# Routed experts: turns of 128 and of 64 slots one by one, two to a loop body

## The chip, the cores and the metric

The kernel runs on one core of a Trainium2 chip. Its engines are TensorE (PE; PEld are its weight loads), VectorE (DVE), ScalarE (ACT), GpSimd (POOL) and SyncE (SP), each with a queue of its own that it works through in order; sixteen DMA engines move data for all of them. The metric is the device time of one execution in microseconds (us).

## What is computed

Two blocks in fp32 on 256 tokens of width 1024. The part at hand is the expert layer of the first block: each token goes to its two best experts of eight, with a gate, an up and a down matrix of 1024 x 3584, 1024 x 3584 and 3584 x 1024 each.

```python
def swiglu(x, w_gate, w_up, w_down):
    return (jax.nn.silu(x @ w_gate) * (x @ w_up)) @ w_down

def moe_swiglu(xn, w_router, w_gate, w_up, w_down):
    xt = xn.reshape(-1, d)
    logits = (xt @ w_router).astype(jnp.float32)
    top_vals, top_idx = lax.top_k(logits, TOP_K)
    top_w = jax.nn.softmax(top_vals, axis=-1)
    combine = jnp.sum(jax.nn.one_hot(top_idx, N_EXPERTS, dtype=jnp.float32) * top_w[..., None], axis=1)
    for e in range(N_EXPERTS):
        y = y + combine[:, e:e + 1] * swiglu(xt, w_gate[e], w_up[e], w_down[e])
```

Around it stand a mixer, attention and a dense feed-forward before, and a second block (mLSTM, a linear recurrence, retrieval of single-neuron experts) behind. The change doesn't touch them.

## The kernel before

**Turns.** One expert is one turn. Its weights come as 42 tiles of 128 x 2048 fp32, 1 MB each: for each of seven chunks of 512 columns two of the gate and two of the up matrix, then fourteen of the down matrix. The experts are ranked by their number of tokens (`ranks`, DVE), expert 0 first in any case; `room` gives the first four ranks 128 slots and the others 64. Before, turn and rank are the same thing: turns 0 to 3 are large (128 slots), turns 4 to 7 small (64 slots). `order` tells SP which expert's tiles a turn loads, `turn_place` and `turn_share` hold each token's slot and weight by turn. If an expert has more tokens than its room, `extra_flag` sends the kernel through a second pass over all experts; the profiled execution has no such pass.

**A tile's way.** SP loads it into one of seven places of a ring (`RING`, L1465). ACT copies it to a rounded high part (`round_tile`, L1857), DVE writes the rest as the low part (`low_part`, L2573), PE multiplies with both, and the place is free when PE has marked the tile as used (`wait_used`). ACT and DVE round and split a tile four steps ahead of PE's (`EXP_AHEAD`); within a turn both have the steps of the products written between the tiles by hand, at step j of 42.

**A large turn** (`turn` on PE, `expert` on ACT and DVE) multiplies the token rows, also split in high and low, in three matmuls for each 128 x 512 piece: high by high, high by low, low by high (`parts`, L862 to L864), 504 in all. **A small turn** (`small_expert`) lays the high parts of its 64 rows and their low parts side by side as 128 rows and needs two (`both`, L968 and L969), 336 in all; the two halves are added when the hidden rows are transposed (`fold`, L982).

**Rows in and out.** At step 15 or 18 of a turn DVE makes the list of the next turn's tokens (`slot_lists`); POOL fetches their rows by an indirect DMA (L1570), 128 rows, or 64 where the next turn is small; PE transposes them in the down phase, and DVE splits them into `gathered_parts` (`transposed_tokens`, L2593 and L2595) at step 33 of a large and step 31 of a small turn. At a turn's end ACT scales the result out of PSUM (`ye`), and POOL adds its rows to `y_tokens` in memory (L1578), in one transfer behind a large turn and in two of 64 rows, one after the other, behind a small one. `y_done` counts these transfers, and `rows_added` is the count that a turn waits for.

**Loops.** PE and ACT run the four large turns in one hardware loop and the small ones in a second (ACT with the last one outside); DVE has the last large turn outside, as it prepares 64 rows. Between the loops each reads `extra_flag` into a register. POOL and SP have their turns written out.

## Time and profile before

| | us |
|---|---|
| median of 3 runs | 2575.92 |
| lowest and highest | 2570.8 and 2578.6 |
| the profiled execution, its span on the core | 2569.7 |

The profile tells of one execution, and its span is the time of that execution on the core; the spread of the three runs is 7.8 us. PE is busy for 93% of the span, DVE 78%, ACT 49%; a busy PE is not PE at its peak, as matmuls overlap in the records. The expert layer takes about a third of the span. Views of the trace used here: the busy time of each engine in given stretches, the waits of an engine, the DMA issues with their time to landing, the rows of one engine in order of time (start, duration, line, operation, what it writes and reads; in brackets the idle time before it and what ended it), and groups of instructions by shape.

### The profile page before, as it was taken

The numbers are of one execution on the slowest core, as the hardware profiler recorded it, in microseconds if no ns is written. First come the engines' busy times: TensorE is split into PE (matmuls) and PEld (weight loads), VectorE is DVE, ScalarE is ACT, GpSimd is POOL, SyncE is SP. The second block draws the span as 40 slices with busy tenths as digits, with TensorE's granted clock in tenths as the row PEclk, the third lists the DMA queues.
The fourth block names the chain that finished last, engine by engine and source line by source line (L and its number), as shares of the span: only waits on it lengthen the run. The fifth ranks groups of instructions, "written<-read, shape, count | busy, mean of one in ns | idle before, by whom it ended". The sixth has DMA issues, their size and how long they took to land.

```text
span 2569.7 us, 32436 instructions
## 1 busy us (share of the span) xinstructions
PE 2384.0 (93%) x12064; PEld 1861.5 (72%) x12064; DVE 2009.7 (78%) x3035; ACT 1256.6 (49%) x1302; POOL 285.7 (11%) x305
## 2 busy tenths in 40 slices
PE   9999999999999999999899899999999987878786
PEld 8899999899788888877677678888985443323332
DVE  5766754865898888989999999666668887887875
ACT  2554332363777777878888886216421111111111
POOL 0000000000000000000000000000013433333341
PEclk9999999999999999999999999999999998899999
DMA  8454654541899999999999997531769999999997
GB/s 246 155 189 133 196 193 140 164 159 67 334 375 380 377 375 370 390 374 415 414 415 408 414 416 265 153 92 47 244 248 421 421 421 421 421 422 421 422 421 294
DMA packets 238447, 786.10 MB, mean 306 GB/s; under 512 B 24369, under 2 KB 154545, under 8 KB 162289
## 3 DMA queue, kind: packets, MB, share of 16 engines
q1 hardware_dynamic: 198000, 504.46, 53.1%
q0 software_dynamic: 39184, 276.58, 26.3%
q10 hardware_dynamic: 1136, 3.43, 0.3%
q8 instruction: 73, 1.20, 0.2%
q14 instruction: 54, 0.43, 0.0%
HBM read 777.08 MB, written 7.34 MB: 305 GB/s over the span
## 4 chain that ended last, share of the span: by engine, by line
PE 58%; DMA 22%; DVE 10%; issue 5%; ACT 4%; POOL 0%; DVEq 0%; ACTq 0%; SPq 0%
DMA dense_weights<-in_peer_rows,work 14%; DMA weight_tiles<-in_moe_tiles 7%; PE banks L862 7%; PE banks L864 7%; PE banks L863 7%; PE banks L728 5%; PE banks L1327 5%; PE banks L682 5%; PE banks L683 4%; PE banks L686 4%; PE banks L660 4%; DVE weight_tiles_low L2573 3%; ACT weight_tiles_high L1857 2%; PE banks L592 1%; PE banks L968 1%
## 5 line engine op out<-in xcount | busy, mean ns | idle before, releaser
L2573 DVE TENSOR_TENSOR weight_tiles_low<-weight_tiles,weight_tiles_high 128x2048 fp32r<-128x2048 f32 x335 | 761.5, 2288 | 72.7 <-ACT weight_tiles_high L1857 67.1
L1857 ACT ACTIVATE weight_tiles_high<-weight_tiles 128x2048 fp32r<-128x2048 f32 x332 | 635.5, 1918 | 149.4 <-DMA weight_tiles<-in_moe_tiles 144.7
L1327 PE MATMUL banks<-dense_weights,work 128*128 128x512 f32 x888 | 415.4, 618 | 57.9 <-DVE work L3104 57.5
L1327 PEld LDWEIGHTS banks<-dense_weights,work 128*128 128x128 f32 x888 | 173.0, 199 | 289.9 <-issue 201.1
L3094 DVE CUSTOM_DVE_ANT_0 dense_weights<-dense_weights,banks 128x1024 f32<-128x1024 f32 x222 | 266.5, 1217 | 68.2 <-DMA dense_weights<-in_peer_rows,work 67.3
L2205 DVE TENSOR_TENSOR weight_tiles_low<-weight_tiles,weight_tiles_high 128x2048 fp32r<-128x2048 f32 x93 | 212.2, 2289 | 129.2 <-ACT weight_tiles_high L1623 129.0
L2119 ACT ACTIVATE work<-work,small 128x2 f32<-128x2 f32 x129 | 38.1, 295 | 540.4 <-DVE work L3094 540.2
L1599 POOL DMA_INDIRECT dense_weights<-in_peer_rows,work x222 | 208.6, 940 | 588.0 <-DVE work L3050 315.0
L968 PE MATMUL banks<-weight_tiles_high,gathered_parts 128*128 128x512 f32 x448 | 183.8, 410 | 27.3 <-DVE weight_tiles_low L2573 26.8
L1623 ACT ACTIVATE weight_tiles_high<-weight_tiles 128x2048 fp32r<-128x2048 f32 x93 | 177.4, 1910 | 56.2 <-PE banks L864 29.5
L682 PE MATMUL banks<-weight_tiles_high 128*128 128x256 f32 x800 | 189.4, 281 | 5.1 <-issue 3.1
L683 PE MATMUL banks<-weight_tiles_high,weight_tiles_low 128*128 128x256 f32 x800 | 187.8, 280 | 0.0
L862 PE MATMUL banks<-weight_tiles_high,gathered_parts 128*128 128x512 f32 x448 | 176.4, 394 | 1.6 <-DVE gathered_parts L2584 1.1
L969 PE MATMUL banks<-weight_tiles_low,gathered_parts 128*128 128x512 f32 x448 | 175.6, 392 | 0.0
L864 PE MATMUL banks<-weight_tiles_high,gathered_parts 128*128 128x512 f32 x448 | 174.7, 390 | 0.0
L863 PE MATMUL banks<-weight_tiles_low,gathered_parts 128*128 128x512 f32 x448 | 174.4, 389 | 0.0
L682 PEld LDWEIGHTS banks<-weight_tiles_high 128*128 128x128 f32 x800 | 152.7, 191 | 5.7 <-issue 3.3
L683 PEld LDWEIGHTS banks<-weight_tiles_high,weight_tiles_low 128*128 128x128 f32 x800 | 152.6, 191 | 0.2
L968 PEld LDWEIGHTS banks<-weight_tiles_high,gathered_parts 128*128 128x128 f32 x448 | 84.0, 188 | 68.9 <-DVE weight_tiles_low L2573 52.8
L3104 DVE TENSOR_SCALAR work<-ident,work 128x128 f32<-128x128 f32 x256 | 79.2, 355 | 46.6 <-ACT work L2119 45.0
L1570 POOL DMA_INDIRECT work<-x_tokens,lists x8 | 18.0, 2248 | 848.0 <-DVE lists L2606 848.0
L728 PE MATMUL banks<-normed,weight_tiles 128*128 128x256 f32 (+1 forms) x512 | 111.7, 380 | 0.0
(508 smaller groups left out, 4467.9 us busy)
## 6 DMA issues: line engine op xcount, KB each, us to landing
weight_tiles<-in_moe_tiles SPq DMA_DIRECT2D x336, 1024.0 KB, 8.3
weight_tiles<-in_w_in SPq DMA_DIRECT2D x38, 1024.0 KB, 5.5
weight_tiles<-in_w_xkv SPq DMA_DIRECT2D x16, 1024.0 KB, 5.7
weight_tiles<-in_ffn_w_gate SPq DMA_DIRECT2D x11, 1024.0 KB, 5.3
weight_tiles<-in_ffn_w_up SPq DMA_DIRECT2D x11, 1024.0 KB, 5.3
weight_tiles<-in_ffn_w_down SPq DMA_DIRECT2D x11, 1024.0 KB, 5.0
weight_tiles<-in_w_xq SPq DMA_DIRECT2D x8, 1024.0 KB, 5.2
weight_tiles<-in_w_xo SPq DMA_DIRECT2D x8, 1024.0 KB, 5.2
```

Source lines behind the costliest of these rows:

```text
L682: pe.matmul(o, high[:, k, n_], high_x(k), start=(k == 0 and i == 0), stop=False)
L683: pe.matmul(o, low[:, k, n_], high_x(k), start=False, stop=False)
L728: mm = pe.matmul(bank[0:m, i * SEQ:(i + 1) * SEQ], w[:, k, i * P:i * P + m], x(k), start=(k == 0), stop=(k == KT - 1))
L862: pe.matmul(o, a_high, b_high, start=start, stop=False)
L863: pe.matmul(o, a_high, b_low, start=False, stop=False)
L864: return pe.matmul(o, a_low, b_high, start=False, stop=stop)
L968: pe.matmul(o, pairs, high, start=start, stop=False)
L1327: mm = pe.matmul(halves[half], diag[(first + j) % 8], pair_row(first + j)[:, 1, half * 512:(half + 1) * 512], start=False, stop=end and j ...
L1857: act.activation(high_tile(j), raw_tile(j), ACT.Copy).then_inc(g.high, 1)
L2205: dve.tensor_tensor(low_tiles[:, n % RING, 0:size], raw_tiles[:, n % RING, 0:size], high_tiles[:, j % HIGH_RING, 0:size].bitcast(F32), ALU ...
L2573: dve.tensor_tensor(low_tile(j), raw_tile(j), high_tile(j).bitcast(F32), ALU.subtract).then_inc(g.split, 1)
L3094: ins = dve.tensor_tensor_reduce(u_row, u_row, tokens(b), 1.0, 0.0, ALU.mult, ALU.add, dots[:, c:c + 1])
```

## The change

The eight turns run as large, small, large, small and so on. Rank r of the first four gets turn 2r, rank r of the last four turn 2r - 7 (`turn_back`, `turn_at`, two steps more in `ranks`). Each engine runs a loop of three bodies, each of one large and one small turn, and then one pair outside, in front of which `extra_flag` is read. `Turn` carries the counts that waits need: the turn's number, the pair's, and how many tile parts came before; `following` gives the turn whose first tiles are rounded and split ahead. `NATIVE` is empty, so `whole` is false everywhere and the branches on it are not taken. The row fetch and the split of rows now follow the new neighbours: a small turn prepares 128 rows, a large one 64. SP's loads and their waits stay as they were; the order of experts comes out of `order`.

```diff
+PAIRS = N_EXP // 2
+NATIVE = ()
+PAIR_PARTS = 2 * EXP_TILES - len(NATIVE)
+class Turn:
+    def parts(self, j):
+        return self.parts_before + j + 1 - (sum(i <= j for i in NATIVE) if self.small else 0)
+    def following(self):
+        if self.pair is None:
+            return plain_turn(self.e + 1)
+        return large_turn(self.pair + 1) if self.small else small_turn(self.pair)
+def large_turn(p):
+    return Turn(p * 2, p * PAIR_PARTS, p, False)
+def small_turn(p):
+    return Turn(p * 2 + 1, p * PAIR_PARTS + EXP_TILES, p, True)
...
-        def rows_added(e, small=True):
-            if small:
-                return 16 * (CLEARS + LARGE + 2 * (e - LARGE))
-            return 16 * (CLEARS + e)
+        def rows_added(pair, small):
+            return pair * 48 + 16 * (CLEARS + (1 if small else 0))
...
-                    with pe.Fori(0, LARGE) as e:
-                        turn(e, False)
+                    with pe.Fori(0, PAIRS - 1) as p:
+                        turn(large_turn(p))
+                        turn(small_turn(p))
                     pe.wait_ge(routing_ready, 1)
                     overflow = pe.value_load(extra_flag[0:1, 0:1], min_val=0, max_val=1)
-                    with pe.Fori(LARGE, N_EXP) as e:
-                        turn(e, True)
+                    turn(large_turn(PAIRS - 1))
+                    turn(small_turn(PAIRS - 1))
...
-                kind, m = "s_" if e >= LARGE else "", HALF if e + 1 >= LARGE else P
+                kind, m = ("s_", P) if e % 2 else ("", HALF)
...
-                with act.Fori(0, LARGE) as e:
-                    expert(e, True)
+                with act.Fori(0, PAIRS - 1) as p:
+                    expert(large_turn(p), True)
+                    small_expert(small_turn(p), True)
...
-                step.then(dve.tensor_tensor(holds, eight(rank, 1), eight(iota8, 2), ALU.is_equal))
+                step.then(dve.tensor_scalar(turn_back, rank, float(LARGE) - 0.5, -float(N_EXP - 1), ALU.is_gt, ALU.mult))
                 step.now(dve.tensor_scalar(room, rank, float(LARGE) - 0.5, float(P - HALF), ALU.is_lt, ALU.mult))
-                step.then(dve.tensor_scalar(room, room, float(HALF), None, ALU.add))
+                step.now(dve.scalar_tensor_tensor(turn_at, rank, 2.0, turn_back, ALU.mult, ALU.add))
+                step.then(dve.tensor_tensor(holds, eight(turn_at, 1), eight(iota8, 2), ALU.is_equal))
+                step.now(dve.tensor_scalar(room, room, float(HALF), None, ALU.add))
...
-                            transposed_tokens(e, done, "s_gather", True)
+                            transposed_tokens(e, done, "s_gather", False)
...
-                            transposed_tokens(e, done, "gather", next_small)
+                            transposed_tokens(e, done, "gather", True)
```

DVE at step 31 of a small turn in the loop, before: two of four banks of PSUM with the next turn's rows become high parts (CAST) and low parts (TENSOR_TENSOR) in `gathered_parts`, 64 rows wide.

```order
L2593 CAST gathered_parts<-banks 128x2x64 [waits pe_group_done]
L2594 ISA
L2595 TENSOR_TENSOR gathered_parts<-banks,gathered_parts 128x2x64 [waits experts_x_rounded]
L2610 REGISTER_ALU
L2593 CAST gathered_parts<-banks 128x2x64 [waits pe_group_done]
L2594 REGISTER_ALU
L2595 TENSOR_TENSOR gathered_parts<-banks,gathered_parts 128x2x64 [waits experts_x_rounded]
```

The same place in the small turn of the loop after (L2651 and L2653 are the same two steps):

```order
L2651 CAST gathered_parts<-banks 128x256 [waits pe_group_done]
L2652 ISA
L2653 TENSOR_TENSOR gathered_parts<-banks,gathered_parts 128x256 [waits experts_x_rounded]
L2670 REGISTER_ALU
L2651 CAST gathered_parts<-banks 128x256 [waits pe_group_done]
L2652 REGISTER_ALU
L2653 TENSOR_TENSOR gathered_parts<-banks,gathered_parts 128x256 [waits experts_x_rounded]
```

Place and order are the same; each step is 256 elements long in place of 2 x 64. Two more such pairs follow in either.

ACT at the end of the last large turn before, with the loop's branch and the load of the flag: L1931 scales the large turn's result, L1857 rounds the small turn's fifth tile.

```order
L1931 ACTIVATE work<-banks,lists 128x512 [waits pe_group_done]
L1903 REGISTER_ALU
L1931 ACTIVATE work<-banks,lists 128x512 [waits pe_group_done]
L1943 REGISTER_ALU
L1943 COMPARE_AND_BRANCH
L1946 TENSOR_LOAD extra_flag [waits routing_ready]
L1946 ISA x2
L1947 UNCONDITIONAL_BRANCH
L1947 ISA
L1856 ISA [waits experts_tile_used]
L1857 ACTIVATE weight_tiles_high<-weight_tiles 128x2048 [waits expert_tile_loaded4]
```

After, the end of a large turn inside the loop's body (L1985 scales, L1907 rounds, L1917 copies the small turn's first gate rows):

```order
L1985 ACTIVATE work<-banks,lists 128x512 [waits pe_group_done]
L1957 REGISTER_ALU
L1985 ACTIVATE work<-banks,lists 128x512 [waits pe_group_done]
L594 REGISTER_ALU
L1907 ACTIVATE weight_tiles_high<-weight_tiles 128x2048 [waits expert_tile_loaded4,experts_tile_used]
L1913 ISA
L1917 ACTIVATE work<-banks 128x512 [waits pe_group_done]
```

The branch and the flag's load are gone from between a large and a small turn.

PE at the end of the small turn in the loop after, where the branch and the flag's load now stand, and the first matmuls of a large turn behind them (L893 to L895 are the three matmuls of `parts`, L1004 and L1005 the two of `both`):

```order
L1004 MATMUL banks<-weight_tiles_high,work_parts 128x512
L1005 MATMUL banks<-weight_tiles_low,work_parts 128x512
L969 REGISTER_ALU
L1104 REGISTER_ALU [waits dve_took]
L1104 COMPARE_AND_BRANCH
L1108 TENSOR_LOAD extra_flag [waits routing_ready]
L1108 ISA x2
L893 MATMUL banks<-weight_tiles_high,gathered_parts 128x512 [waits experts_tiles_split,act_took]
L894 MATMUL banks<-weight_tiles_low,gathered_parts 128x512
L895 MATMUL banks<-weight_tiles_high,gathered_parts 128x512
```

Before, this place had the end of a large turn in front of it and a small turn behind:

```order
L864 MATMUL banks<-weight_tiles_high,work_parts 128x512
L937 REGISTER_ALU
L1057 REGISTER_ALU [waits dve_took]
L1057 COMPARE_AND_BRANCH
L1060 TENSOR_LOAD extra_flag [waits routing_ready]
L1060 ISA x2
L1061 UNCONDITIONAL_BRANCH
L1061 ISA
L957 ISA [waits act_took]
L968 MATMUL banks<-weight_tiles_high,gathered_parts 128x512 [waits experts_tiles_split]
L969 MATMUL banks<-weight_tiles_low,gathered_parts 128x512
```

The flag is read between a small and a large turn in place of a large and a small one.

## Rows read from the trace of the kernel before

**Rows 1.** The page: span; DMA issues: count, KB, us to landing.

```profile
span 2569.7 us, 32436 instructions
...
weight_tiles<-in_moe_tiles SPq DMA_DIRECT2D x336, 1024.0 KB, 8.3
```

**Rows 2.** Busy us by turn, L1, L3 to S7; last: clock, DMA share, rate.

```profile
775.43:894.84 119.41, 119.41 (x549) 99.09 (x548) 107.25 (x74) 93.97 (x68) 3.01 (x2) 1.00 0.96 377
...
1014.26:1133.67 119.41, 119.41 (x550) 99.10 (x548) 107.01 (x75) 94.52 (x69) 5.08 (x2) 1.00 0.98 377
1133.67:1239.32 105.65, 97.30 (x465) 77.10 (x463) 96.99 (x73) 88.09 (x70) 4.52 (x2) 0.98 1.01 412
1239.32:1347.58 108.26, 98.05 (x465) 75.36 (x465) 102.22 (x75) 91.92 (x72) 6.41 (x3) 1.00 1.01 414
1347.58:1455.91 108.33, 98.06 (x464) 75.42 (x464) 102.18 (x75) 91.91 (x72) 6.36 (x3) 1.00 1.01 413
1455.91:1564.58 108.67, 97.94 (x463) 76.79 (x464) 99.97 (x74) 87.96 (x70) 6.32 (x3) 0.98 0.95 387
```

**Rows 3.** Waits of PE, 1133.67 to 1564.58: us in total, times, longest.

```profile
PE banks L968 <- DVE weight_tiles_low L2573: 37.9, 60, 2.2
```

**Rows 4.** DMA issues of 1020:1110 (L) and 1260:1340 (S), us to landing.

```profile
weight_tiles<-in_moe_tiles SPq DMA_DIRECT2D x32, 1024.0 KB, 5.4
...
weight_tiles<-in_moe_tiles SPq DMA_DIRECT2D x30, 1024.0 KB, 10.6
```

**Rows 5.** DVE in order of time, end of L3 and end of S4.

```profile
1124.51 2.29 DVE L2573 TENSOR_TENSOR weight_tiles_low<-weight_tiles,weight_tiles_high 128x2048 fp32r<-128x2048 f32 x1 [0.44 <-ACT weight_tiles_high L1857]
...
1223.78 15.49 DVE L2573 TENSOR_TENSOR weight_tiles_low<-weight_tiles,weight_tiles_high 128x2048 fp32r<-128x2048 f32 x7
```

**Rows 6.** PE in order of time: L0, first matmuls of S4 and S5.

```profile
666.76 0.50 PE L862 MATMUL banks<-weight_tiles_high,gathered_parts 128*128 128x512 f32 x1 [0.55 <-DVE weight_tiles_low L2573]
...
1133.67 0.39 PE L968 MATMUL banks<-weight_tiles_high,gathered_parts 128*128 128x512 f32 x1
...
1239.32 0.50 PE L968 MATMUL banks<-weight_tiles_high,gathered_parts 128*128 128x512 f32 x1
```

**Rows 7.** ACT in order of time: fetch in L2, start and fetch in S4.

```profile
956.38 1.93 ACT L1857 ACTIVATE weight_tiles_high<-weight_tiles 128x2048 fp32r<-128x2048 f32 x1
...
963.13 1.92 ACT L1857 ACTIVATE weight_tiles_high<-weight_tiles 128x2048 fp32r<-128x2048 f32 x1 [0.57 <-DMA weight_tiles<-in_moe_tiles]
...
1144.57 1.92 ACT L1857 ACTIVATE weight_tiles_high<-weight_tiles 128x2048 fp32r<-128x2048 f32 x1 [2.38 <-DMA weight_tiles<-in_moe_tiles]
1148.59 1.92 ACT L1857 ACTIVATE weight_tiles_high<-weight_tiles 128x2048 fp32r<-128x2048 f32 x1 [2.10 <-DMA weight_tiles<-in_moe_tiles]
...
1185.94 1.92 ACT L1857 ACTIVATE weight_tiles_high<-weight_tiles 128x2048 fp32r<-128x2048 f32 x1
...
1192.36 1.91 ACT L1857 ACTIVATE weight_tiles_high<-weight_tiles 128x2048 fp32r<-128x2048 f32 x1 [0.26 <-DMA weight_tiles<-in_moe_tiles]
```

**Rows 8.** DVE groups by shape, 656 to 1570: count, busy us, mean ns.

```profile
L2655 DVE TENSOR_TENSOR work<-banks,work 128x512 f32<-128x512 f32 x28 | 19.1, 683 | 0.0
...
L2595 DVE TENSOR_TENSOR gathered_parts<-banks,gathered_parts 128x128 fp32r<-128x128 f32 x20 | 5.8, 291 | 0.7
L2593 DVE CAST gathered_parts<-banks 128x128 fp32r<-128x128 f32 x20 | 5.6, 281 | 0.0
L2595 DVE TENSOR_TENSOR gathered_parts<-banks,gathered_parts 128x256 fp32r<-128x256 f32 x12 | 5.1, 425 | 0.4
L2593 DVE CAST gathered_parts<-banks 128x256 fp32r<-128x256 f32 x12 | 5.0, 415 | 0.0
```

**Rows 9.** DVE in order of time, a step of the ranks.

```profile
660.17 0.17 DVE L2499 TENSOR_SCALAR small<-small 128x8 f32<-128x8 f32 x1
```

**Rows 10.** ACT in order of time, head of the loop body, L1.

```profile
781.37 1.28 ACT L1907 ACT_TABLE_LOAD   x1
782.67 0.60 ACT L1907 ACTIVATE work<-banks 128x512 f32<-128x512 f32 x1
```

More of the change, by code:

```diff
@@ L93, with __init__, whole, plain_turn @@
 EXP_MARKS = 2 * CHUNKS + DOWN - 1
+PAIRS = N_EXP // 2
+NATIVE = ()
+PAIR_PARTS = 2 * EXP_TILES - len(NATIVE)
+class Turn:
+    def __init__(self, e, parts_before, pair, small):
+        self.e, self.parts_before, self.pair, self.small = e, parts_before, pair, small
+    def whole(self, j):
+        return self.small and j in NATIVE
+    def parts(self, j):
[8 more added lines that the diff above has]
+    return Turn(p * 2 + 1, p * PAIR_PARTS + EXP_TILES, p, True)
+def plain_turn(e):
+    return Turn(e, e * EXP_TILES, None, False)
 class Groups:
@@ L393, in two_blocks @@
         turn_place, turn_share = turn_place_all[:, :, 0:N_EXP], pairs_of(32)
-        rank_key, rank, excess, order_f = (std_row[:, 8 * i:8 * i + 8] for i in range(4))
+        rank_key, rank, excess, order_f, turn_back, turn_at = (std_row[:, 8 * i:8 * i + 8] for i in range(6))
         def by_rank(a):
@@ L930, in gather, with turn @@
                         g.end(mm, (key, i))
-                def turn(e, small):
+                def turn(t):
+                    e, small = t.e, t.small
                     g.begin_turn(e)
@@ L989, in turn @@
                             for half in range(2):
-                                high, low = split(4 * c + 2 * n_ + half, KT // 2)
+                                j = 4 * c + 2 * n_ + half
+                                if t.whole(j):
+                                    whole = unsplit(j, KT // 2)
+                                else:
+                                    high, low = split(j, KT // 2)
                                 for i in range(KT // 2):
                                     k = half * (KT // 2) + i
-                                    if small:
+                                    if t.whole(j):
+                                        mm = pe.matmul(bank, xe_high[:, k, :].bitcast(F32), whole[:, i, :], start=(k == 0), stop=(k == KT - 1))
+                                    elif small:
                                         mm = both(bank, xe_high[:, k, :], high[:, i, :], low[:, i, :], k == 0, k == KT - 1)
@@ L1011, in turn @@
                             halves.append(g.begin("a", (down_, 1)))
-                        high, low = split(GATE_UP + d, 2)
+                        if t.whole(GATE_UP + d):
+                            whole = unsplit(GATE_UP + d, 2)
+                        else:
+                            high, low = split(GATE_UP + d, 2)
                         for i in range(2):
@@ L1016, in turn @@
                                 n_ = slice(h * 512, (h + 1) * 512)
-                                if small:
+                                if t.whole(GATE_UP + d):
+                                    mm = pe.matmul(halves[h], he_pairs[:, f, :].bitcast(F32), whole[:, i, n_], start=(f == 0), stop=(f == ET - 1))
+                                elif small:
                                     mm = both(halves[h], he_pairs[:, f, :], high[:, i, n_], low[:, i, n_], f == 0, f == ET - 1)
@@ L1899, in small_expert, with expert @@
                         took_it(act.activation(ye[:, h * 512:(h + 1) * 512], bank_in(("s_down", h))[:, :], ACT.Copy, scale=share_here))
-                def expert(e, follow):
+                def expert(t, follow):
+                    e = t.e
                     def done(key):
@@ L2568, in expert_places, with low_part @@
                     ins.then_inc(g.weighted_now_ready, 1)
[L2570 to L2572 removed]
+                def low_part(t, j):
+                    if t.whole(j):
+                        return
+                    dve.wait_ge(g.high, t.parts(j))
                     dve.tensor_tensor(low_tile(j), raw_tile(j), high_tile(j).bitcast(F32), ALU.subtract).then_inc(g.split, 1)
```

95 lines of the change are left out of this document (50 added, 45 removed).

## The prediction

> **What bounds the kernel now.** I read the page first: its own span is 2569.7 us, and the transfer that counts is the one of the expert tiles, 336 loads of 1 MB each [rows 1]. The eight turns that use them are a third of the span, and the change touches nothing else. Then I cut that stretch at the first matmul of each turn, because the eight turns are of two kinds and a mean over them says nothing [rows 2]. Call a turn of 128 slots L and one of 64 slots S; the kernel before runs L0 L1 L2 L3 S4 S5 S6 S7. The reader is to see two limits. An L lasts 119.41 us and PE is busy for all of it, while the transfers run at 377 GB/s. An S lasts 108.3 us (S5, S6), the transfers run at 413 to 414 GB/s with a share of 1.01, and PE is busy 98 us. So L is bound by PE and S by the tile stream. The waits say the same: between 1133.67 and 1564.58 PE waited 37.9 us, in 60 waits, for the low parts of tiles [rows 3], and in the same view of 775.43 to 1133.67 there is no row at all. A transfer lands 5.4 us after its issue in an L and 10.6 us in an S [rows 4]: in an L the ring of seven tiles is full and each load waits for PE to free its place; in an S the loads queue behind one another.
>
> The third reading is the cushion. DVE starts the low part of the first tile of S4 at 1124.51 and needs 2.29 us [rows 5], and PE takes that tile at 1133.67 [rows 6]: it had lain ready for 6.9 us. At the end of S4 DVE writes seven low parts without a pause, to 1239.27 [rows 5], and PE starts S5 at 1239.32 [rows 6]: no cushion. An L fills it, an S empties it. L turns are not shortened by a cushion, since PE is busy throughout; only an S behind an L is, as it can start on tiles that are there. S4 is the one such turn of the trace and lasts 105.65 us, 2.6 less than S5.
>
> **The change part by part.** The order becomes L0 S1 L2 S3 L4 S5 L6 S7.
>
> *Four S turns behind an L in place of one.* Each is taken from S4, 105.65 us. Why S4 gains only 2.6 of its 6.9 us can be seen on ACT: its tiles at 1144.57 and 1148.59 came late, ACT having stood idle 2.38 and 2.10 us for them [rows 7]. That is the moment when the 128 rows of L3's result are added in memory, and it comes behind every L, so I keep the cost in the price.
>
> *L turns behind an S.* Three of them (L2, L4, L6) start without a cushion. PE still needs 119.41 us if tiles are never late: 2.84 us a tile on the mean, while tiles come every 108.3 / 42 = 2.58 us, ACT is busy 94.52 and DVE 107.01 us of the 119.41 of L3 [rows 2]. All three suppliers are faster than PE, so the lag grows from zero and PE should not wait. The excess over a whole L is 119.4 - 108.3 = 11.1 us, more than the 6.9 that the ring holds, so the cushion is full again at its end, as before S4. Price 0.
>
> *Rows of the next turn.* While an S runs, DVE now writes the gathered rows of an L: four copies and four differences of 128x256 in place of 128x128. From the two shapes [rows 8] that is 4 x (0.415 - 0.281) + 4 x (0.425 - 0.291) = 1.07 us more. It stands ahead of the seven low parts that reach without a pause to the turn's end [rows 5], so nothing hides it, and PE of the next L starts 1.07 us later. In an L it is 1.07 us less, and hidden. S7 runs it too, but nothing follows that needs it. Price 3 x 1.07.
>
> *The fetch of those rows* is now of 128 rows in an S and 64 in an L. In an S it competes with the tile stream. Across a fetch of 64 rows two tiles took 1192.36 - 1185.94 = 6.42 us, across one of 128 rows, in L2, 963.13 - 956.38 = 6.75 [rows 7]. The difference is 0.33; since the stream in L2 was not full, I take 0.4 and keep 0 to 1.3 (as much again as the smaller fetch costs: 6.42 less two tiles of 2.58). Four S turns: 1.6 us. In an L it is hidden behind PE.
>
> *Ranks to turns.* Two small DVE steps more, ahead of the low parts of L0. A step of that size takes 0.17 us [rows 9], and each holds the next one up; PE was waiting for the low part behind them, 0.55 us [rows 6], so they are on the path: I take 0.4 us for both.
>
> *Loops.* Each engine runs a body of two turns three times and then one pair outside, in place of two loops. The register steps stay one a wait. ACT has two table loads at the head of the body, each of 1.28 us (the second at 781.37, [rows 10]); they came in L0 to L3 and now come in L0, L2 and L4. Before, the cushion hid them. In L2 and L4 it is gone, but PE reaches its seventh tile 6 x 2.84 = 17.0 us into the turn and that tile arrives 6 x 2.58 = 15.5 us behind the first, so by then 1.5 us of a load are covered, and ACT has its own idle time, a fifth of the turn, for the rest. I take 0 and keep up to 2.6 us in each of the two turns.
>
> **Sum.** L0 stands first in both, with 0.4 us more for the ranks. The other seven before: 3 x 119.41 + 105.65 + 108.26 + 108.33 + 108.67 = 789.1 us. After: L2, L4, L6 3 x 119.41; S1, S3, S5 3 x (105.65 + 1.07 + 0.4) = 321.4; S7 105.65 + 0.4 + 0.4 (it ended that much later than S5 and S6) = 106.4. That is 358.2 + 321.4 + 106.4 = 786.0, and with the 0.4 of L0 the change is worth 2.7 us less. The profiled execution's span of 2569.7 would become 2567.0; the median of the runs shown, 2575.92, lies 6.2 above that span, and I put the same difference on it: 2573.2 us. A measurement of this kernel tells about 0.3%, 7.7 us, from no change, so the forecast is that no difference is seen.
>
> One rule speaks against the change. In rows: S4 and S7 show a granted clock of 0.98 over the turn, L1 to L3 1.00 [rows 2], which is 2.1 us of full-speed work lost at the lower level, 1.2 GHz; in an S PE's idle 10 us cover that. The Trainium skill, page "TensorE: Matmul & The Clock Gate", section "HAM oscillation — how this bites in real kernels", has it that a matmul stream which waits for its transfers falls back to the half clock again and again. The trace agrees for two of four S turns, for none of the L turns. By that rule an L that starts behind waits could carry such a fall, where nothing covers it: 3 x 2.1 = 6.3 us more than my sum.
>
> **Rivals.**
> *Smoothing as a whole (faster).* If the ring let the loads run on through every L, each pair would go at the stream's pace, 2 x 108.3 + 0.4 = 217.0 instead of 119.41 + 107.12 = 226.5; three pairs give 28.5 us, and the time 2544.7. Against it: 6.9 us of cushion where 11.1 would be needed, and an L that PE fills. Half way stands the case that the late tiles of S4 [rows 7] were peculiar to it: two of those us back in each of four S turns make 2565. Chance of either 0.15.
>
> *The start of L chokes (slower).* Without a cushion, PE, ACT and DVE may wait for each other in the first chunks of an L: the silu and the product, 0.60 us [rows 10] and 0.68 us (19.1 us over 28, [rows 8]), fall on the path once a chunk. With three chunks in each of L2, L4, L6 that is 9 x 1.28 = 11.5, with both table loads in L2 and L4 5.1 more: 2573.2 + 16.6 = 2589.8. For it: ACT is at 94.52 and DVE at 107.01 of 119.41, so little slack, and the trace has no L without a cushion but L0, which started from a ring loaded ahead. Against it: both are faster than PE over a chunk. It decides from the point where low parts follow each other more slowly than PE's 2.84 us a tile. Chance 0.16.
>
> *Clock (no change that is seen).* The fall of the clock in three L turns, as above: 2579.5. Chance 0.08.
>
> *It doesn't do what it says.* If the new places of experts put more than 64 rows into an S, the second pass over all experts runs, eight L turns more, over 900 us. The room of an expert still follows its rank, so 0.01.
>
> **How the numbers follow.** The forecast, 2573.2, holds 0.60; its own bounds are 0 to 1.3 for each of four fetches and 0 to 2.6 for two turns' loads, so about 2571.6 to 2582. Faster by over 0.3% are the smoothing cases, 0.15; slower the choke and the second pass, 0.17; within 0.3% the forecast and the clock, 0.68. For eight in ten the range takes in the half-way smoothing (2565, with 2 us for the spread of runs) and most of the choke: 2563 to 2587.
>
> **What would show it.** In the trace after, the windows by turn should read near 119.4 for L2, L4, L6 with PE busy throughout, and near 107 for S1, S3, S5; transfers in S near 412 GB/s, in L 370 to 380. The waits of PE should lie in the S turns alone. DVE's last low part of an S should end where PE's L starts. An S below 103 would show that the cushion is worth more than S4 says; waits of PE in the first dozen tiles of an L, or an L above 121, that the choke is real; a clock under 1.00 in an L, the third rival. A time below 2568 or above 2584 would make the sum wrong.

## Result and profile after

The changed kernel takes 2586.81 us (median of 5 runs, 2584.21 to 2592.36) against 2577.27 us for the kernel before in the same session. The ratio that the runs give is 1.0047, 95% interval 1.0031 to 1.0063 (the two medians alone give 1.0037): slower, by 8 to 16 us. The forecast was 2573.2 us and no difference that is seen.

The page of the changed kernel, its span, its instruction fetch (packets, MB, share of 16 engines) and its tile loads:

```profile
span 2590.6 us, 32249 instructions
...
q8 instruction: 101, 1.65, 0.3%
...
weight_tiles<-in_moe_tiles SPq DMA_DIRECT2D x336, 1024.0 KB, 7.8
```

The loads are the same 336 as in [rows 1]. The fetch of instructions was 73 packets and 1.20 MB before. The amount alone is not the loss: the written-out kernels below fetch 97 packets and don't show it.

The turns of the changed kernel, L0 S1 L2 S3 L4 S5 L6 S7, in the view of [rows 2] (us of the turn, busy us of PE, PEld, DVE, ACT, POOL; then the granted clock, the DMA share and GB/s):

```profile
661.09:781.90 120.81, 119.88 (x549) 99.12 (x550) 112.50 (x105) 89.39 (x65) 2.17 (x1) 1.00 0.92 354
781.90:893.07 111.17, 97.95 (x466) 78.19 (x464) 102.90 (x75) 92.22 (x73) 4.92 (x2) 0.97 1.01 409
893.07:1014.13 121.06, 121.06 (x548) 100.30 (x549) 104.79 (x73) 91.84 (x67) 7.46 (x3) 0.99 0.97 368
1014.13:1125.70 111.57, 97.16 (x465) 76.96 (x464) 104.71 (x76) 94.08 (x75) 5.16 (x2) 0.98 1.01 410
1125.70:1248.15 122.45, 122.45 (x548) 101.25 (x549) 106.79 (x74) 93.15 (x67) 7.46 (x3) 0.97 0.96 364
1248.15:1355.66 107.51, 98.03 (x466) 78.55 (x464) 98.03 (x73) 89.27 (x71) 4.40 (x2) 0.97 1.01 408
1355.66:1475.23 119.57, 119.57 (x549) 99.16 (x549) 109.47 (x75) 93.05 (x67) 14.18 (x3) 1.00 1.00 385
1475.23:1583.21 107.98, 97.59 (x464) 77.95 (x463) 97.03 (x73) 84.97 (x69) 5.14 (x2) 0.97 0.93 378
```

Read it in pairs. The last pairs do what was forecast: L0 120.81, S5 107.51, L6 119.57. S1 and S3 are 4 us longer than S5, and L2 and L4, which stand behind them, 1.5 and 2.9 us longer than L6. The eight turns sum to 922.1 us, against 909.6 before. That is 12.6 us, about what the ratio gives for the whole loss (12.1). Of the rest of the difference between the two spans, 6.1 us lie ahead of L0, where the code is the same (L0 starts anywhere from 653.4 to 661.1 in the kernels below), and 2.3 us behind S7.

The place of the loss is the seam between S3 and L4. PE in order of time there (start, duration, line, operation, in brackets the idle time before it):

```profile
1120.20 0.39 PE L1004 MATMUL banks<-weight_tiles_high,work_parts 128*128 128x512 f32 x1
1120.43 0.40 PE L1005 MATMUL banks<-weight_tiles_low,work_parts 128*128 128x512 f32 x1
1125.70 0.79 PE L893 MATMUL banks<-weight_tiles_high,gathered_parts 128*128 128x512 f32 x1 [4.87 <-ACT work L1951]
1126.29 0.63 PE L894 MATMUL banks<-weight_tiles_low,gathered_parts 128*128 128x512 f32 x1
```

PE stands for 4.87 us between the last matmul of S3 and the first of L4. The view names ACT's L1951, but a releaser is inferred: the name is that of the event that came last, and an experiment below shows the same first matmul starting 3.3 us ahead of L1951. Meanwhile something else took time: the branch that closes PE's loop. The line of PE's loop in the changed kernel (L1104) and in the kernel before (L1057); PEldq is PE's own queue, and the columns are the count, ns min/median/max and the first and last start:

```profile
L1104 PEldq COMPARE_BRANCH  x3: 76/6222/6477, 886.5 to 1353.6; - x3
```

```profile
L1057 PEldq COMPARE_BRANCH  x4: 76/210/244, 771.6 to 1129.8; - x4
```

The branch that falls out of the loop takes 76 ns in both. A taken one took 0.21 to 0.24 us before and takes 6.2 and 6.5 us now. There are two, at 886.5 (S1 to L2) and at 1118.9 (S3 to L4). The last is over at 1125.38, and L4's first matmul starts at 1125.70. What follows is seen in the granted clock (last columns: clock, DMA share, GB/s) just behind either stop:

```profile
893.07:896.30 3.23, 3.23 (x8) 2.56 (x9) 1.99 (x1) 0.74 (x3) 2.23 (x1) 0.50 0.99 413
896.30:905.00 8.70, 8.70 (x40) 7.21 (x39) 4.49 (x2) 8.66 (x6) 2.42 (x2) 1.00 0.87 247
...
1125.70:1131.80 6.10, 6.10 (x14) 4.78 (x15) 1.75 (x1) 3.52 (x4) 2.46 (x1) 0.50 0.86 271
1131.80:1140.00 8.20, 8.20 (x37) 6.76 (x36) 7.15 (x4) 7.46 (x6) 2.23 (x1) 1.00 0.87 284
```

L2 begins with 3.2 us and L4 with 6.1 us at 1.2 GHz, then comes 2.4 GHz. About half of such a stretch is lost, and the two turns are 1.5 and 2.9 us longer than L6.

### The profile page after: what moved, and what is told of

Read it like the earlier page. It is cut to its first block, busy times and chain, and to the rows that moved or that the text cites. A ratio compares the mean times of both kernels' runs of the same rounds, so it can differ in the third digit from the quotient of the medians.

```text
span 2590.6 us, 32249 instructions
## 1 busy us (share of the span) xinstructions
PE 2396.5 (93%) x12064; PEld 1879.7 (73%) x12064; DVE 2012.4 (78%) x3037; ACT 1254.5 (48%) x1300; POOL 300.8 (12%) x305
## 4 chain that ended last, share of the span: by engine, by line
PE 60%; DMA 20%; DVE 10%; issue 5%; ACT 4%; POOL 0%; DVEq 0%; ACTq 0%; SPq 0%
DMA dense_weights<-in_peer_rows,work 14%; PE banks L893 7%; PE banks L895 7%; PE banks L894 7%; DMA weight_tiles<-in_moe_tiles 6%; PE banks L759 5%; PE banks L1375 5%; PE banks L713 5%; PE banks L714 5%; PE banks L717 5%; PE banks L691 4%; DVE weight_tiles_low L2631 3%; ACT weight_tiles_high L1907 1%; PE banks L1004 1%; PE banks L1005 1%
## 5 line engine op out<-in xcount | busy, mean ns | idle before, releaser
L1907 ACT ACTIVATE weight_tiles_high<-weight_tiles 128x2048 fp32r<-128x2048 f32 x332 | 635.4, 1917 | 147.7 <-DMA weight_tiles<-in_moe_tiles 141.9
L1004 PE MATMUL banks<-weight_tiles_high,gathered_parts 128*128 128x512 f32 x448 | 182.7, 408 | 21.8 <-DVE weight_tiles_low L2631 21.7
L893 PE MATMUL banks<-weight_tiles_high,gathered_parts 128*128 128x512 f32 x448 | 178.9, 399 | 12.1 <-DVE weight_tiles_low L2631 5.8
L1005 PE MATMUL banks<-weight_tiles_low,gathered_parts 128*128 128x512 f32 x448 | 176.5, 394 | 0.0
L895 PE MATMUL banks<-weight_tiles_high,gathered_parts 128*128 128x512 f32 x448 | 176.2, 393 | 0.0
L1004 PEld LDWEIGHTS banks<-weight_tiles_high,gathered_parts 128*128 128x128 f32 x448 | 84.8, 189 | 56.1 <-DVE weight_tiles_low L2631 36.8
```

The lines of the kernel that those rows point to most:

```text
L893: pe.matmul(o, a_high, b_high, start=start, stop=False)
L895: return pe.matmul(o, a_low, b_high, start=False, stop=stop)
L1004: pe.matmul(o, pairs, high, start=start, stop=False)
L1907: act.activation(high_tile(j), raw_tile(j), ACT.Copy).then_inc(g.high, 1)
```

## Experiments

**Theory:** PE's loop body of one L and one S (2191 recorded instructions from branch to branch, against 1181 for an L and 1014 for an S before) is more than PE keeps, so each taken back-edge (the branch from the end of the body to its start) waits for its code. The counts are of records, of which a few can be missing: the same L body reads 1177 to 1181. **Rival:** the L turns that start without a cushion stop by themselves, as the choke in the prediction, and the branch's duration only shows that. All ratios are to the kernel before and come from 11 or 12 executions of each kernel (the changed one: 5); the turns are read from the one that was profiled. Four more kernels below have one execution each and no ratio.

| kernel | eight turns, us | ratio, 95% interval |
|---|---|---|
| before | 909.6 | 1 |
| changed kernel | 922.1 | 1.0047, 1.0031 to 1.0063 |
| PE's pairs written out | 914.5 | 1.0007, 0.9996 to 1.0018 |
| hint for PE's back-edge | 913.7 | 1.0014, 1.0002 to 1.0025 |
| body of S and then L | 913.3 | 1.0014, 1.0000 to 1.0028 |
| order of before, two turns a body | 916.0 | 1.0020, 1.0010 to 1.0031 |
| PE's and ACT's pairs written out | 907.5 | 0.9998, 0.9989 to 1.0007 |
| before, PE's and ACT's loops written out | 911.2 | 1.0008, 0.9999 to 1.0017 |
| PE and ACT written out, early skip hint | 909.9 | 0.9981, 0.9972 to 0.9991 |
| before, early skip hint | 909.5 | 1.0000, 0.9991 to 1.0010 |

### PE's pairs written out

```diff
-                    with pe.Fori(0, PAIRS - 1) as p:
+                    for p in range(PAIRS - 1):
```

> Theory (long body): PE's body of one L and one S is some 2190 instructions, more than PE holds, so each of the two taken back-edges (S1 to L2, S3 to L4) waits for code; the branch records of 6.2 and 6.5 us are that wait. Rival (bare start): an L behind an S has no cushion, and the stop of 4 to 5 us at its start is the wait of PE, ACT and DVE for each other, with any loop. Here PE's four pairs are written out one behind the other, with no loop on PE; ACT, DVE and the order of the work stay. Long body: S1 and S3 fall from 111.2 and 111.6 to about 107.5 (S5 of the same kernel, which has no taken back-edge behind it), L2 and L4 from 121.1 and 122.5 to about 119.6 (L6), the eight turns from 922.1 to about 910 us, and the time stands to the kernel before as 1.000 (0.998 to 1.002). Bare start: the turns stay at 921 to 923 us, ratio 1.0047.

Most of the loss is gone: 1.0007, an interval that holds 1. PE at the start of L4, and the wait that is left in that turn:

```profile
1115.02 0.47 PE L893 MATMUL banks<-weight_tiles_high,gathered_parts 128*128 128x512 f32 x1 [0.19 <-DVE weight_tiles_low L2631]
...
1127.73 0.47 PE L893 MATMUL banks<-weight_tiles_high,gathered_parts 128*128 128x512 f32 x1 [1.55 <-DVE weight_tiles_low L2631]
```

The stop at the seam is 0.19 us in place of 4.87, and S1 and S3 read 106.81 and 107.48 us. But L2 and L4 did not fall to 119.6: they read 123.64 and 121.43, and the turns sum to 914.5 us, not 910. Both contain a wait some 11 us in, 2.23 and 1.55 us, and L2 a fall of the clock right behind it. ACT at that place in L4:

```profile
1118.34 1.25 ACT L1951 ACTIVATE work<-banks,lists 128x512 f32<-128x512 f32 x2
1122.05 1.28 ACT L1907 ACT_TABLE_LOAD   x1 [2.46 <-issue]
1123.34 3.71 ACT L1907 ACTIVATE weight_tiles_high<-weight_tiles 128x2048 fp32r<-128x2048 f32 x2
1127.07 1.28 ACT L1961 ACT_TABLE_LOAD   x1
```

Behind L1951 ACT is idle for 2.46 us ("issue": it waited for nothing that the view shows) and then loads a table before it rounds the tile that PE will miss.

ACT's own queue (ACTq) shows where the idle time comes from. Its taken back-edge in the kernel before (L1943, at the end of L0) and here (L1997, between S3 and L4), each with the record that follows it, the first of the body:

```profile
L1943 ACTq COMPARE_BRANCH  x1: 54/54/54, 775.7 to 775.7; - x1
L1943 ACTq FUSED_REGOPS  x1: 59/59/59, 776.0 to 776.0; - x1
```

```profile
L1997 ACTq COMPARE_BRANCH  x1: 45/45/45, 1116.9 to 1116.9; - x1
L1997 ACTq FUSED_REGOPS  x1: 68/68/68, 1121.9 to 1121.9; - x1
```

Before, 0.2 us lie between the two; here it is 4.9 us, and 4.9 to 5.1 us at every taken back-edge of ACT's pairs, in the changed kernel too. ACT's body has 337 recorded instructions, and had 162 to 178. So ACT's back-edge has the same wait as PE's, only that it doesn't show in the branch's own record. DVE's body of 287 instructions has none: 0.3 us, as before. That ACT waits for code is concluded from the likeness, and from the wait's going away with the loop (below); a hint on ACT was not tried.

### A hint for PE's back-edge

```diff
-                    with pe.Fori(0, PAIRS - 1) as p:
+                    with nc.Fori(0, PAIRS - 1, engines=[pe.engine], hint_back_edge=True) as p:
```

> The changed kernel with its loops as they are, but with a prefetch hint for the back-edge as the first instruction of PE's body. Long body: the two taken branches fall from 6.2 and 6.5 us to under 0.5 us, S1 and S3 to about 107.5, L2 and L4 to about 119.6, the turns to 910 to 911 us, ratio 1.000 (0.998 to 1.002). Bare start: nothing changes, since the same instructions wait for the same tiles: 921 to 923 us, ratio 1.0047.

One instruction more at the head of the body, and the branches read:

```profile
L1104 PEldq COMPARE_BRANCH  x3: 80/367/409, 884.8 to 1343.7; - x3
```

S1 and S3 are 106.82 and 107.35 us, as with the loop written out; L2 and L4, at 121.84 and 121.38, keep the wait at 11 us. The order of the work, the tiles and the waits are those of the changed kernel, and only the fetch of the branch's target is different; its amount is that of the changed kernel (100 packets against 101). The rival has no room here. The turns, 913.7 us, miss the 910 to 911 expected by that wait.

### The body cut at the other place

```diff
+                    turn(large_turn(0))
                     with pe.Fori(0, PAIRS - 1) as p:
-                        turn(large_turn(p))
                         turn(small_turn(p))
+                        turn(large_turn(p + 1))
...
-                    turn(large_turn(PAIRS - 1))
                     turn(small_turn(PAIRS - 1))
```

> The changed kernel's order of turns, with PE's body cut at the other place: L0 ahead of the loop, three bodies of S and then L, S7 behind. The body is as long as before the cut, but its two taken back-edges now lie between L2 and S3 and between L4 and S5, where PE leaves an L with tiles lying ready and enters a turn in which it idles 10 us anyway. Long body: the two branch records still last 6 to 6.5 us, L2 and L4 read 123 to 125 us (the stop counts to the turn it ends), but S3 and S5 get most of it back (103 to 105 us), S1 reads 107.5, and the turns sum to 910 to 913 us, ratio 1.000 to 1.002. Bare start: the L turns behind S turns still stop at their start, S1, S3 and S5 read 111 us, and the sum stays at 921 to 923 us, ratio 1.0047.

The branches last 5.44 and 5.99 us, now at the ends of L2 and L4. Turns L2 to S5:

```profile
886.20:1009.79 123.59, 120.15 (x549) 98.85 (x549) 111.61 (x76) 98.21 (x72) 8.27 (x4) 1.00 0.99 380
1009.79:1114.62 104.83, 96.15 (x465) 75.74 (x465) 96.53 (x72) 87.03 (x69) 3.69 (x2) 1.00 1.01 413
1114.62:1238.44 123.82, 120.10 (x549) 98.84 (x549) 111.56 (x76) 98.05 (x72) 8.02 (x4) 1.00 0.99 378
1238.44:1345.09 106.65, 98.51 (x465) 78.38 (x465) 96.60 (x73) 86.67 (x69) 4.42 (x2) 0.97 1.00 403
```

The same wait for code costs less here, for two reasons. Its stop is 1.69 us at the end of L2 and 2.23 at the end of L4, not 4.64 and 4.87: in an L PE's sequencer runs some 4 us ahead of its matmuls, and in an S, which waits for tiles, only 1.9 us (from the branch's start to the end of the last matmul). And the S behind it gets part of the stop back (S3 as expected, S5 less). The sum of 913.3 us is a little over the 910 to 913 expected, since L2 and L4 also hold 1.75 and 1.48 us of the wait for ACT's late tile.

### The order of before, two turns a body

```diff
-                    with pe.Fori(0, LARGE) as e:
-                        turn(e, False)
+                    with pe.Fori(0, LARGE // 2) as p:
+                        turn(p * 2, False)
+                        turn(p * 2 + 1, False)
...
-                    with pe.Fori(LARGE, N_EXP) as e:
-                        turn(e, True)
+                    with pe.Fori(LARGE // 2, N_EXP // 2) as p:
+                        turn(p * 2, True)
+                        turn(p * 2 + 1, True)
```

> The kernel before, in its own order (four L, then four S), with PE's loops of two turns a body: L L is some 2360 instructions, S S some 2030. No L stands behind an S. Long body: the one taken back-edge behind L1 waits, its branch record is 6 to 6.5 us in place of 0.21, L1 or L2 grows by 4 to 5 us, and up to 3 us more if the clock falls behind the stop; the back-edge between S5 and S6 may wait or not (2030 is about what PE holds) and costs nothing or little there, because an S has 10 us of idle PE. Eight turns 913.5 to 917.5 us in place of 909.6, ratio 1.0015 to 1.003. Bare start: the order is that of before, all L turns have their cushion: 909.6 us, ratio 1.000, branch records 0.2 us.

Here nothing is interleaved. The branch behind L1 takes 5.70 us, the one behind S5 6.18:

```profile
L1057 PEldq COMPARE_BRANCH  x2: 83/2892/5700, 896.2 to 1138.8; - x2
```

```profile
L1062 PEldq COMPARE_BRANCH  x2: 79/3128/6177, 1355.7 to 1574.7; - x2
```

L1 grew by 2.1 us and L2, behind the stop, by 1.7 at the lower clock: less than expected, as the sequencer's lead hides 4 us in an L. The S side was a miss: S5 grew by 5.1 us, and S6 gave back only 2.6. Together 6.4 us and 1.0020. A long body alone makes the kernel before slower.

### Where the wait begins

```diff
+                                    if thin:
+                                        mm = pe.matmul(bank, xe_high[:, k, :], high[:, i, :], start=(k == 0), stop=(k == KT - 1))
...
-                        turn(p * 2, True)
+                        turn(p * 2, True, True)
```

> Where the wait of a taken back-edge begins. The kernel before with two turns a body on PE, as in the third run, whose S S body of 2026 recorded instructions waited 6.2 us at its back-edge; here the first S of each body leaves out the product with the low part of its 28 gate and up tiles (PE's work alone; the tiles are still loaded, rounded and split), which makes the body about 1800 instructions. If what counts is whether the body as a whole is still held (2048 instructions by the Trainium skill, page Runtime: NRT & Kernel Launch, section Instruction fetch mechanics), the branch takes 0.2 us, and the 2026 waited only for its place against the blocks of 256. If PE holds less, it still takes 5 to 6.5 us. The L L body, unchanged, waits 5.7 us as it did.

> As the run before it, with that product left out in both S turns of a body: about 1580 instructions. Held as a whole: 0.2 us at the back-edge between S5 and S6. If PE holds less than that: 5 to 6.5 us, and the bound lies between this and the 1181 instructions of the L body of the kernel before, whose back-edge took 0.21 us.

The back-edge between S5 and S6, first with one S made thinner (1804 recorded instructions), then with both (1576), one execution each:

```profile
L1064 PEldq COMPARE_BRANCH  x2: 79/3094/6109, 1354.6 to 1572.9; - x2
```

```profile
L1064 PEldq COMPARE_BRANCH  x2: 76/156/236, 1356.8 to 1573.0; - x2
```

In this kernel the bound lies between 1576 and 1804 recorded instructions. By the Trainium skill, page "Runtime: NRT & Kernel Launch", section "Instruction fetch mechanics", TensorE's instruction memory takes 2048 instructions in blocks of 256, and a taken branch whose target isn't in the "current 2-page window" waits for a fetch. The runs agree that such a wait is there and depends on the body's length. They don't agree with either figure: two blocks would be 512 instructions, and bodies of 1014 to 1576 looped without a wait; bodies of 2026 and 1804, under 2048, waited. Why the bound lies there, and whether a body's place against the blocks counts, was not tried.

### ACT's pairs written out as well

```diff
-                with act.Fori(0, PAIRS - 1) as p:
+                for p in range(PAIRS - 1):
```

> With PE's pairs written out, L2 and L4 still lasted 123.6 and 121.4 us in place of L6's 119.5: PE waited 2.2 and 1.6 us, 11.1 us into the turn, for one tile. Theory (table loads): ACT's loop body begins with two table loads of 1.28 us, and without a cushion they make that tile late; L6 stands behind the loop and has none. Rival (boundary work): the copies of the S turn's result on ACT, and what else lies at every S to L boundary, make it late. Here ACT's four pairs are written out too, which takes the table loads out of L2 and L4 and leaves the rest. Table loads: L2 and L4 fall to 119.5 to 119.7 us with no such wait, the turns to 908 to 910 us from 914.5, ratio to the kernel before 0.998 to 1.000. Boundary work: L2 and L4 stay at 121 to 123.6 us and the ratio at 1.0007.

Turns L2, S3, L4 and the sum:

```profile
881.30:1000.87 119.57, 119.57 (x548) 99.17 (x549) 110.43 (x76) 94.26 (x68) 6.73 (x3) 1.00 1.00 389
1000.87:1107.28 106.41, 96.66 (x466) 76.97 (x464) 98.06 (x73) 88.40 (x71) 4.46 (x2) 0.98 1.01 409
1107.28:1226.85 119.57, 119.57 (x549) 99.16 (x549) 111.21 (x76) 94.66 (x68) 8.49 (x3) 1.00 0.99 389
...
sum 907.53, PE 866.38 PEld 705.82 DVE 835.36 ACT 721.20 POOL 42.07; mean PE 108.30 PEld 88.23 DVE 104.42 ACT 90.15 POOL 5.26
```

All three L turns behind an S last 119.57 us, with PE busy for all of it, no wait above 0.2 us, and the clock at 1.00. The head of ACT's loop made the late tile. Writing the loop out takes away the table loads and the wait at the back-edge together, so the run doesn't tell them apart, and the expectation had only the loads in mind. The rows of the kernel with PE alone written out give an estimate: had ACT gone on 2.46 us earlier in L4 and 2.54 us earlier in L2, the tile that PE missed by 1.55 and 2.23 us would have been there in time, table load and all.

### ACT written out alone

> The changed kernel with ACT's pairs written out and PE's loop kept: what made L2 and L4 of the changed kernel 1.5 and 2.9 us longer than L6. Clock: the stop of PE at the taken back-edge (records of 6.2 and 6.5 us) is followed by 3.41 to 6.83 us at the granted clock of 0.5, and the table loads lie under the stop. Then L2 and L4 stay at 121 to 122.5 us, S1 and S3 at 111.2 to 111.6, the turns sum to 920 to 922. Table loads: without them L2 and L4 fall to 119.6 and the turns to 917.5 to 918.

The edit is the last one, on the changed kernel with PE's loop kept, in one execution. L2 and L4:

```profile
886.76:1007.93 121.17, 121.17 (x548) 100.35 (x549) 106.68 (x75) 90.82 (x65) 5.50 (x3) 0.99 0.98 368
1120.92:1242.83 121.91, 121.91 (x548) 100.91 (x549) 106.74 (x74) 91.21 (x66) 6.58 (x3) 0.98 0.97 366
```

They stay long, with PE busy throughout and the clock at 0.99 and 0.98. S1 and S3 read 111.95 and 112.99, the sum 923.5 (expected 920 to 922, S1 and S3 being longer here). So in the changed kernel itself the excess of L2 and L4 is the clock's, and ACT's late tile is hidden under PE's stop. It comes to light only when the stop is gone, which is why the first two repairs gave some 8 us and not 12.6.

### The loops of the kernel before

> The kernel before, in its own order, with PE's and ACT's loops written out. It prices the loops of that kernel. If a loop whose body PE holds costs nothing, as its branch records of 0.21 us say, and table loads are covered by the cushion: 909.6 us for the turns, ratio 1.000 (0.999 to 1.001). If the loops do cost there too, 907 us or less and 0.999 or less; then the gain of the written-out interleaved kernel over its looped form would say less about the order.

The edit is the same on PE's and ACT's four loops of the kernel before. 911.2 us and 1.0008: those loops, whose bodies of 1014 to 1181 (PE) and 162 to 178 (ACT) recorded instructions show no wait, cost nothing that is seen.

### The late tiles behind an L

```diff
-                for half in ((slice(0, HALF), slice(HALF, P)) if kind else (slice(0, P),)):
+                for half in ((slice(0, HALF), slice(HALF, P)) if kind else (slice(0, 8),)):
```

> The sixth run's kernel with one thing left out: of the 128 rows of an L turn's result only 8 are added in memory (so the output lacks the other 120). It prices the late tiles that stand behind every L and were kept in the price of an S behind an L, 105.65 us. In the sixth run PE waited 13.4 us into S1, S3, S5, S7 for 0.97, 2.12, 3.06 and 2.74 us. Theory (the add takes room from the tile stream): with 8 rows those waits go to under 0.6 us and the four S turns fall by about 2.2 us on the mean, from 106.9 to 104.5 to 105. Rival (the stream needs that time to get up to speed behind an L, whatever is added): the waits stay at 1 to 3 us and the S turns at 106.4 to 107.9.

The four S turns, in one execution:

```profile
777.13:881.33 104.20, 96.52 (x465) 77.05 (x464) 98.19 (x73) 88.86 (x71) 4.66 (x2) 0.98 1.01 415
...
1000.86:1105.56 104.70, 97.14 (x465) 78.10 (x464) 99.25 (x73) 89.86 (x72) 4.96 (x2) 0.97 1.01 412
...
1225.01:1330.91 105.90, 96.94 (x465) 76.99 (x464) 100.22 (x74) 90.65 (x72) 4.95 (x2) 0.98 1.00 413
...
1450.48:1553.61 103.13, 96.22 (x464) 77.05 (x463) 95.47 (x72) 84.23 (x68) 4.17 (x2) 0.98 0.94 390
```

They sum to 417.9 us in place of 427.7: 2.4 us a turn. The waits some 13 us into the turns fall to 0.84 us or less, a little over the 0.6 expected. The DMA share is 1.00 or 1.01 in S1, S3 and S5 with and without the add, so it takes the stream's time, and what [rows 7] showed of S4 belongs to every S behind an L. (S5 kept a wait of 1.86 us for a tile, later in the turn.)

### The branch behind the turns

```diff
+                    hints.append(pe.mark_branch_hint_location())
                     turn(small_turn(PAIRS - 1))
...
-            skip_hint = pe.mark_branch_hint_location()
+            skip_hint = hints[0]
```

> PE's and ACT's pairs written out as in the sixth run (907.5 us for the eight turns), and the prefetch hint of the branch that skips the second pass moved from behind the last turn to ahead of S7. That branch took 4.10 us in the kernel before and 6.26 in the changed one, 5.44 and 5.43 us after its hint began work in the code right ahead of it; it took 0.48 in one run only. Theory (hint too late): a hint some 70 instructions ahead of its branch comes too late to have the code there, one that stands a turn ahead does not: the branch takes under 0.5 us, the first matmul behind it starts 3.9 us behind the last turn in place of 9.55, and what lies behind the turns takes 1001 us in place of 1005.3; ratio to the kernel before 0.997 to 0.999. Rival (the hint does not serve this branch, or its code is dropped again in S7): 5.8 to 6.5 us as before, ratio 0.9998.

> The kernel before in its own order, with the last S turn of PE's second loop set behind the loop and the same hint ahead of it; ACT's loops stay. It tells the hint's worth from that of the order. Hint too late: the branch falls from 4.10 to under 0.5 us, the eight turns stay at 909.6, ratio 0.998 to 0.9995; the interleaved kernel with the same hint then stands about 2 us below this one, by its turns. Rival: branch at 4 to 6.5 us, ratio 1.000.

(The hint stood 5.03 us ahead of that branch in the kernel before and 6.22 in the changed one; the expectation has these two wrong.) In both kernels the branch does what the first theory expected:

```profile
L1147 PEldq COMPARE_BRANCH  x1: 411/411/411, 1573.3 to 1573.3; - x1
```

```profile
L1100 PEldq COMPARE_BRANCH  x1: 362/362/362, 1574.2 to 1574.2; - x1
```

The time does not: 1.0000 for the kernel before with the early hint. In the interleaved one the first matmul behind the branch starts 5.7 us after the turns in place of 9.55 (expected 3.9, but PE is still at work on the matmuls ahead of it until then), and the 60th matmul behind the turns at 11.1 in place of 16.7. The 100th starts at 20.9 in place of 22.1, and what lies behind the turns takes 1005.5 us in place of 1005.3. The waits of PE in the first 40 us behind the turns show where the lead goes:

```profile
PE banks L713 <- DVE weight_tiles_low L2261: 2.7, 1, 2.7
```

PE arrives early and waits for the next tile's low part. The written-out interleaved kernel with this hint has the lowest ratio of all, 2572.72 us against 2577.79 and 0.9981 (0.9972 to 0.9991): 2.3 to 7.2 us under the kernel before. Where it has its lead over the same kernel without the hint can't be told: its profiled execution took 2577.06 us, the longest of its 12, and shows no gain behind the turns.

## Why the prediction was wrong

**The step that failed is "Loops".** It priced register steps ("stay one a wait") and ACT's table loads ("I take 0 and keep up to 2.6 us in each of the two turns"), and put the back-edges themselves, PE's and ACT's, at nothing without a reason. The part on the change even shows the branch moved to the start of an L. The trace of before held the number, eight branches of PE of 0.08 to 0.24 us, but for bodies of up to 1181 and 1014 instructions, and a body of 2191 was not in it. The two stops of 4.64 and 4.87 us (9.1 more than the 0.18 each that is left without the loop) and the clock behind them (1.5 + 2.9) make 13.5 of the 14.6 us between the changed kernel's turns and the written-out ones, 922.1 and 907.5; the rest, some 1 us, is scatter, above all in S7 (1.3 us longer).

**The table loads** were a suspicion of the right place. The reckoning had the seventh tile at stake, where it is the fifth, 11 us into the turn, and it counted the loads but not the wait at ACT's back-edge ahead of them, of which 2.5 us were idle time. With PE written out, two L turns paid 2.23 and 1.55 us for the two together, and one of them a fall of the clock besides (the rest of its 123.64 us, 1.8). By the estimate above the loads alone would have cost nothing, as forecast; no run has the loads without the wait. In the changed kernel itself PE's own stop hid all of it.

**All other terms held.** With both loops written out the sum of the turns is 907.5 us; the sum in the prediction, 909.6 less 2.7, is 906.9.
- *S behind an L*, with the rows and the fetch 107.1 us: 106.75, 106.41 and 107.85, in sum 321.0 against 321.4. S7: 106.68 against 106.4.
- *L behind an S, price 0*: 119.57 against 119.41, three times. The lag does grow from zero and PE doesn't wait.
- *Rows of the next turn, 1.07 us*: PE's stop for the first of the seven low parts was 2.18 us in S4 before and is 3.34 in S3 of the written-out kernel (2.18 to 2.19 and 3.31 to 3.34 in all four S turns):

```profile
1226.12 0.50 PE L968 MATMUL banks<-weight_tiles_high,work_parts 128*128 128x512 f32 x1 [2.18 <-DVE weight_tiles_low L2573]
```

```profile
1094.07 0.77 PE L1004 MATMUL banks<-weight_tiles_high,work_parts 128*128 128x512 f32 x1 [3.34 <-DVE weight_tiles_low L2631]
```

- *Ranks, 0.4 us*: L0 lasts 120.81 us against 120.40 before, and 121.13 against 120.84 with the loops written out.

**The order by itself**, forecast at 2.7 us less, has no sure number. In the turns of single traces it is 907.5 us against 909.6 before and 911.2 with the loops written out; with the early hint it is 909.9 against 909.5, no gain at all. In the times the written-out kernels have medians of 2574.93 and 2575.22 us, with ratios of 0.9998 and 1.0008 whose intervals overlap; those with the early hint 2572.72 and 2576.62, with ratios of 0.9981 and 1.0000 whose intervals just meet. That agrees with a small gain and shows no size.

**The rivals.** *Choke at the start of L*, 2589.8 us, named nearly the right time for the wrong reason, and it is only for this rival that the stated range, 2563 to 2587, reaches to the measured 2586.81: that the range held is luck. L turns "above 121" were to prove the choke, and they came, but without the two loops there is no wait above 0.2 us at the start of any L behind an S. The mark should have asked what PE waited for. *Clock*: L turns did carry a fall, 1.5 and 2.9 us against 2.1 assumed, but only behind a stop of PE, at its seam or for ACT's late tile; in the written-out kernel L2, L4 and L6 show 1.00, and the S turns, which wait for tiles, 0.97 and 0.98. So the rule that the prediction cites (the Trainium skill, page "TensorE: Matmul & The Clock Gate", section "HAM oscillation — how this bites in real kernels"), of a matmul stream that waits for its transfers, agrees with the S turns; the L turns of the changed kernel fell behind a wait for code. *Smoothing*: the late tiles are not peculiar to S4, as the run with eight rows shows. *Behind the turns* the prediction had no term: the skipping branch took 6.26 us in place of 4.10, and by the 100th matmul PE was 5.0 us later than before, by the end of the span 2.3.

## What to carry to other kernels

When a change makes a loop's body longer, count the body's instructions on each engine, and read how long the loop's branches take and how soon the next record of that queue follows, before pricing the seam at nothing: here a taken back-edge went from 0.2 to over 6 us somewhere between 1576 and 1804 recorded instructions on PE, and from 0.2 to 4.9 us between 178 and 337 on ACT. Such a stop of PE took the clock with it here (1.5 and 2.9 us) and hid smaller delays beside it, so repair one and look again. If the body must be long, write the loop out, arm a hint at its head, or put the seam where the engine runs ahead of itself and the next stretch has slack.

## What the chip showed that was not expected

- A hint 4.9 to 6.2 us and some 70 instructions ahead of its branch mostly left it at 4.1 to 6.5 us; one a turn ahead brought it to 0.36 and 0.41 us. In one kernel, that with both S turns thinner, the near hint gave 0.48 us; why there is open.
- How much of a code wait becomes idle PE depends on how far PE's sequencer is ahead: with branches of 5.4 to 6.8 us the stop was 1.7 to 3.1 us at the end of an L and 4.2 to 4.9 us at the end of an S.
- A code wait need not stand in the branch's record: PE's branch reads 6.2 us, ACT's reads 45 ns with 4.9 us of nothing behind it.
